# A transformer block with mixture-of-experts: the last two experts' rows added by matmuls from a gate matrix, the other pairs read back earlier, two norms from one power step, the mixer's scale folded into its weights

## What is computed

```python
# experts: token t goes to its two best experts of one group
ys = lax.ragged_dot(silu(xs @ w1) * (xs @ w3), w2, group_sizes) * gate   # 512 (token, expert) pairs
ffn = jax.ops.segment_sum(ys, tok, num_segments=256)                     # two rows per token are added
x = x + gate2 * ffn
...
x = rmsnorm(x, final_norm_w)                                             # end of the first block
h = rms_norm(x, norm_mix_g)                                              # second block: a second norm on it
d = causal window means (2, 4, 8, 16 tokens) of h, minus h               # per group of 256 columns
x = x + pool_scale * (einsum('bsgc,gcd->bsgd', d, pool_w) + pool_b)
x = x + conv_ffn(rms_norm(x, norm_ffn_g))                                # 1024 -> 2 x 2816 -> 1024
```

## Time and profile before

| what | value |
| --- | --- |
| median of 3 executions | 1063.36 us (1061.33 to 1064.96) |
| the profiled execution | 1059.67 us, its span 1057.8 us |
| mean granted TensorE clock of it | 0.952 of full speed |
| PE, DVE, ACT, POOL busy | 85%, 35%, 19%, 17% of the span |
| DMA, experts' stage | 1.0 of the 16 engines, some 400 to 415 GB/s |

### The profile page before, as it was taken

One profiled execution on the slowest core, in us unless ns is written; L12 is line 12 of the kernel. 1 busy time (PEld: TensorE's weight loads), 2 busy tenths in 40 slices (PEclk: granted clock), 3 DMA queues, 4 the chain that ended last, 5 costly groups with the idle time before them and its releaser, 6 DMA issues.

```text
span 1057.8 us, 11605 instructions
## 1 busy us (share of the span) xinstructions
PE 894.7 (85%) x4729; PEld 543.5 (51%) x4729; DVE 365.5 (35%) x639; ACT 199.5 (19%) x296; POOL 176.5 (17%) x187
## 2 busy tenths in 40 slices
PE   5679999999955979998887887887887279999998
PEld 2567756774432434433332332332322269999987
DVE  1244412232251242221221211212212566888843
ACT  2106212111130000000000000000000335565532
POOL 0000654011011120111101111011000221323300
PEclk9889999989987998999999999999999579999999
DMA  9898327364595999999999999999994784654511
GB/s 352 207 208 227 110 80 231 88 238 168 199 415 197 401 407 403 402 401 399 409 403 416 415 402 410 404 412 413 405 419 203 261 255 145 204 163 169 213 58 40
DMA packets 90803, 300.25 MB, mean 284 GB/s; under 512 B 12843, under 2 KB 36963, under 8 KB 66039
## 3 DMA queue, kind: packets, MB, share of 16 engines
q1 hardware_dynamic: 82727, 286.63, 72.7%
q10 hardware_dynamic: 2896, 8.58, 2.1%
q0 software_dynamic: 5120, 4.22, 1.4%
HBM read 300.44 MB, written 11.53 MB: 295 GB/s over the span
## 4 chain that ended last, share of the span: by engine, by line
PE 57%; DMA 33%; SPq 3%; issue 2%; DVE 2%; ACT 1%; POOL 1%; ACTq 0%; POOLq 0%; DVEq 0%
DMA arena<-in_w_dram 16%; DMA ring<-in_w_dram 13%; PE ps L421 9%; PE ps L763 7%; PE ps L847 6%; PE ps L849 6%; PE ps L848 6%; PE ps L410 5%; PE ps L766 4%; PE ps L786 3%; PE ps L483 3%; SPq L1874 2%; PE ps L431 2%; DMA rows_scratch<-MX 1%; DMA ring<-in_w_ada_dram 1%
## 5 line engine op out<-in xcount | busy, mean ns | idle before, releaser
L766 PE MATMUL ps<-ring,proj 128*64 128x512 f32 x288 | 134.1, 613 | 24.9 <-DMA ring<-in_w_dram 24.9
L763 PE MATMUL ps<-ring,proj 128*64 128x512 f32 x304 | 143.1, 612 | 1.7 <-issue 1.7
L1235 DVE TENSOR_TENSOR proj<-RQ,ps 64x512 f32<-64x512 f32 x32 | 22.1, 690 | 298.3 <-ACT RQ L1570 288.4
L766 PE MATMUL ps<-arena,proj 128*64 128x512 f32 x224 | 100.9, 596 | 20.6 <-DMA arena<-in_w_dram 20.6
L1570 ACT ACTIVATE RQ<-ps 64x512 f32<-64x512 f32 x32 | 18.9, 591 | 472.2 <-PE ps L766 472.2
L1800 POOL DMA_INDIRECT pair_scratch<-MX,idx x32 | 32.4, 1014 | 423.7 <-DVE MX L1249 423.7
L847 PE MATMUL ps<-h_h,w_h 128*128 128x256 f32 x352 | 100.8, 286 | 1.6 <-DVE h_l L1331 1.6
L849 PE MATMUL ps<-h_h,w_l 128*128 128x256 f32 x352 | 100.5, 286 | 0.0
L848 PE MATMUL ps<-h_l,w_h 128*128 128x256 f32 x352 | 100.5, 286 | 0.0
L421 PE MATMUL ps<-ring,hT 128*128 128x512 f32 x224 | 99.7, 601 | 0.8 <-ACT hT L1522 0.8
L763 PE MATMUL ps<-arena,proj 128*64 128x512 f32 x208 | 95.1, 596 | 1.9 <-issue 1.9
(11 more groups left out here) (285 smaller groups left out, 1377.6 us busy)
## 6 DMA issues: line engine op xcount, KB each, us to landing
ring<-in_w_dram SPq DMA_DIRECT2D x108, 1024.0 KB, 28.0
arena<-in_w_dram SPq DMA_DIRECT2D x84, 1024.0 KB, 28.1
ring<-in_w_ada_dram SPq DMA_DIRECT2D x12, 2048.0 KB, 10.0
ring<-in_ffn_w_in_dram SPq DMA_DIRECT2D x22, 1024.0 KB, 7.7
ring<-in_w_in_dram SPq DMA_DIRECT2D x8, 2048.0 KB, 22.3
ring<-in_ffn_w_out_dram SPq DMA_DIRECT2D x5, 2048.0 KB, 8.1
ring<-in_w_out_dram SPq DMA_DIRECT2D x2, 2048.0 KB, 9.8
rows_scratch<-MX ACTq DMA_DIRECT2D x4, 512.0 KB, 11.5
```

Source lines behind the costliest of these rows:

```text
L763: pe.matmul(ps[0:SLOTS, :], XTe[i % 2][:, k, :], u1[:, k, :], start=(k == 0), stop=(k == 7))
L766: t = pe.matmul(ps[64:64 + SLOTS, :], XTe[i % 2][:, k, :], u3[:, k, :], start=(k == 0), stop=(k == 7))
```

## The change

The last two experts (30 and 31) are no longer scattered. In the `aside` DVE builds from the slots and the gates a matrix `spread` (tokens by slots, for each of the two experts and each half of the tokens), PE transposes it, and DVE copies it out (`spread_t`). After `down(31)` PE multiplies `spread_t` by the buffers `YS`, eight matmuls with 64 rows of contraction, into four PSUM banks, and DVE adds these to `X`. The other pairs are read back by ACT once expert 29's rows have landed, ahead of `silu(31)`, into slot 0 of `ring`, and DVE adds them within the experts' loop: the first half of the tokens ahead of its `down(30)`, the second ahead of its `down(31)`. Since rows of the last two experts' pairs are never written, both scratch tensors are zeroed in the first part by eight transfers of 512 KB from a zeroed row buffer.

The second norm's sum is expressed by the first's, so that POOL takes both powers in one instruction on two columns. The preparations (L1660 before) move to DVE. POOL multiplies `pool_w` by the scale, in place, behind the powers, and DVE's separate multiplication goes. Bands and `pool_w` share slot 1 and are loaded as soon as `up(30)` has used it. Two matmuls of 128 columns become one of 256.

```diff
             for blk in range(1, NBLK):
                 places(blk)
+            ps = take("spread")
+            pe.wait_ge(spread_ready, 1)
+            for j in range(2):
+                for n in range(2):
+                    i = pe.transpose(ps[:, 256 * j + 128 * n:256 * j + 128 * n + 128], spread[:, j, n, :], ident)
+            i.then_inc(*mm.up("spread"))
...
+            acc = {(n, q): take("x2", n, q) for n in range(2) for q in range(2)}
+            for j, i in enumerate(LAST):
+                pe.wait_ge(*drained("down", i))
+                for n in range(2):
+                    for q in range(2):
+                        r = slice(64 * q, 64 * q + 64)
+                        t = pe.matmul(acc[n, q][:, :], spread_t[r, j, n, :], YS[i % 4][r, :], start=(j == 0), stop=(j == 1))
+                        if j:
+                            t.then_inc(*mm.up("x2", n, q))
...
-                pe.matmul(ps[:, 0:128], MX[:, 0, cc], band[:, g, 0:128], start=True, stop=True)
-                pe.matmul(ps[:, 128:256], MX[:, 0, cc], band[:, g, 128:256], start=True, stop=False)
+                pe.matmul(ps[:, 0:256], MX[:, 0, cc], band[:, g, 0:256], start=True, stop=False)
...
             def aside():
                 ve.tensor_copy(fcol, full("fcol")[:, 0:192]).then_inc(*free("fcol"))
+                for n in range(2):
+                    for k in range(2):
+                        ve.tensor_scalar(share[:, n, k, :], flat[k][:, n, NE - 2:NE], gate[:, k, n:n + 1], None,
+                                         ALU.mult).then_inc(*vd.up())
+                ve.wait_ge(*vd.now())
+                for j in range(2):
+                    for n in range(2):
+                        for k, to in enumerate((spread, spread_2)):
+                            ve.tensor_scalar(to[:, j, n, :], cst("places"), slot[:, k, n:n + 1], share[:, n, k, j:j + 1],
+                                             ALU.is_equal, ALU.mult).then_inc(*vd.up())
+                ve.wait_ge(*vd.now())
+                ve.tensor_tensor(spread, spread, spread_2, ALU.add).then_inc(spread_ready, 1)
                 for blk in range(1, NBLK):
                     places(blk)
+                ve.tensor_copy(spread_t, full("spread")[:, :].rearrange("p (e n t) -> p e n t", e=2, n=2)).then_inc(*free("spread"))
...
+                if add_pairs and i in LAST:
+                    add_pairs(i - LAST[0], (pairs_in[i - LAST[0]], 32))
                 down(i)
...
+            second_residual(0)
+            second_residual(1)
+            mean_squares(0)
+            both_norms(0)
+            mean_squares(1)
+            both_norms(1)
...
+                    ve.tensor_tensor(X[:, n, gs], X[:, n, gs], full("pooled", n, gg)[:, :], ALU.add).then_inc(*free("pooled", n, gg))
+            for n in range(2):
+                ve.wait_ge(third_sq, n + 1)
+                ve.tensor_scalar(tms[n][0][:, 0:1], ss[:, n:n + 1], 1.0 / 1024, 1e-6, ALU.mult, ALU.add).then_inc(*vd.up("x3_mean", n))
             for n in range(2):
                 newton(rr[:, n:n + 1], [q[:, 0:1] for q in tms[n]])
...
+            def main_pairs():
+                all_scattered(ac, main, NE - 2)
+                read_pairs(ys, pairs_in)
...
+                if pairs and i == N - 1:
+                    pairs()
                 ac.wait_ge(*E.mm.of("up", i))
...
+            for n in range(2):
+                po.wait_ge(*vd.of("means", n))
+                root(tms[n][1][:, 0:2], pair_m[n])
+            w_pool = mixer_weights()[1].rearrange("p (g c) d -> p g c d", c=2)
+            po.wait_ge(*filled(("mixer",)))
+            po.tensor_tensor(w_pool, w_pool, v_psc.rearrange("p (g d) -> p g d", g=4).unsqueeze(2).to_broadcast(
+                [128, 4, 2, 256]), ALU.mult).then_inc(pool_scaled, 1)
...
+            sp.wait_ge(row_zeroed, 1)
+            for i in range(4):
+                for pairs in (ys, ys_more):
+                    sp.dma_start(pairs.rearrange("(p a) c -> p (a c)", p=128)[:, 1024 * i:1024 * i + 1024],
+                                 v_pb).then_inc(pairs_zeroed, 16)
             load_ada(4)
...
-            sp.wait_ge(pairs_in[1], 32)
-            sp.wait_ge(pairs_in[0], 32)
...
+            s, _ = units.at["mixer",]
+            sp.wait_ge(*used(units.before["mixer",]))
```

More of the change, by code:

```diff
@@ L721, in tensor_program @@
                 pe.wait_ge(*more.mm.now())
+                for b in range(8):
+                    pe.wait_ge(more.bank_free[b], more.banks.count[b])
+            acc = {(n, q): take("x2", n, q) for n in range(2) for q in range(2)}
[7 more added lines that the diff above has]
+                            t.then_inc(*mm.up("x2", n, q))
             tensor_last(pe, take)
@@ L1207, in vector_program, with vector_experts @@
             with ve.If(some > 0):
-                vector_experts(ve, more, None)
-                ve.wait_ge(*more.drained("down", len(more.jobs) - 1))
+                vector_experts(ve, more, None, None)
+                ve.wait_ge(more_pairs_in, 64)
+                for n in range(2):
+                    for k in range(2):
+                        ve.scalar_tensor_tensor(X[:, n, :], YP[:, k, n, :], gate[:, k, n:n + 1], X[:, n, :], ALU.mult,
+                                                ALU.add).then_inc(*more_vd.up())
+                        ve.wait_ge(*more_vd.now())
             vector_last(ve, full, free, newton)
-        def vector_experts(ve, E, aside):
+        def vector_experts(ve, E, aside, add_pairs):
             def full(*name):
@@ L1255, in vector_experts @@
             else:
[L1256 to L1257 removed]
+                all_scattered(ve, main, NE - 2)
             turn_x(0)
@@ L1282, in add_second, with mixer_weights, second_residual @@
+        def mixer_weights():
+            w = slots[units.at["mixer",][0]]
+            return w[:, 0:1536].rearrange("p (g c) -> p g c", g=4), w[:, 2048:4096].rearrange("p (a b) -> p a b", b=256)
+        def vector_last(ve, full, free, newton):
+            def second_residual(n):
+                for q in range(2):
+                    xq = X[:, n, 512 * q:512 * q + 512]
+                    ve.tensor_tensor(xq, xq, full("x2", n, q)[:, :], ALU.add).then_inc(*free("x2", n, q))
                 ve.wait_ge(finals_in, 48)
+                ve.wait_ge(*drained("x2", n, 0))
+                ve.wait_ge(*drained("x2", n, 1))
@@ L1781, in gpsimd_program @@
                 gpsimd_experts(po, more, None)
-                for i in range(4):
-                    po.wait_ge(more.scattered[i], 16 * (len(more.jobs) // 4))
-            for i in range(4):
-                po.wait_ge(main.scattered[i], 16 * (NE // 4))
-            po.memset(mark, 0.0).then_inc(joined, 1)
-            gpsimd_last(po, row_power, power)
+                all_scattered(po, more, len(more.jobs))
+            all_scattered(po, main, NE - 2)
+            gpsimd_last(po)
         def gpsimd_experts(po, E, aside):
@@ L1817, in gpsimd_experts, with gpsimd_last, root @@
                     gather(i + 4)
-                scatter(i)
+                if E is main and i == 0:
+                    po.wait_ge(pairs_zeroed, 128)
+                if E is more or i not in LAST:
+                    scatter(i)
                 if aside and i == 3:
                     aside()
-        def gpsimd_last(po, row_power, power):
-            def again(n):
-                po.wait_ge(*vd.of("norm_once", n))
-                power(1.0 / 1024, 1e-6, sv[:, n:n + 1], [q[:, 4:5] for q in tms[n]])
-            row_power("x2_sq", 0, n=0)
-            again(0)
-            row_power("x2_sq", 1, n=1)
-            again(1)
+        def gpsimd_last(po):
+            def root(y, m):
+                po.tensor_tensor(y, m, half.to_broadcast([128, m.shape[1]]), ALU.pow).then_inc(pow_ready, 1)
+            for n in range(2):
+                po.wait_ge(*vd.of("means", n))
[4 more added lines that the diff above has]
+                [128, 4, 2, 256]), ALU.mult).then_inc(pool_scaled, 1)
             src = ffn_part(0)
```

164 lines of the change are left out of this document (80 added, 84 removed).

## The result

The changed kernel takes 1064.89 us (median of 19 runs, 1062.78 to 1070.9), the kernel before beside it 1061.57 us (19 runs, 1056.27 to 1066.22). The ratio is 1.0034, with a 95% interval of 1.002 to 1.0047: the change costs 3.6 us, between 2.1 and 5.0. The forecast was +4.3 us, and with it 1067.7 us (range 1059 to 1072); the level is 2.8 us too high, most of it because the 1063.36 us it starts from, the median of three executions, lie 1.8 us above the median of 19.

What follows compares the result with a forecast made beforehand. The weight stream bounds the experts' stage, then a serial chain up to the feed-forward part; +4.6 (aside) - 0.85 (join) + 0.5 + 0.1 = +4.3 us on 1063.36 gives 1067.7 us, range 1059 to 1072.

Steps and rivals of the forecast that it cites:

- What bounds it, first part: Weight stream bounds the experts' stage; eight more transfers early on cost zero, up to 10.5 us if uncovered.
- The aside: Behind down(3), the matrix work makes PE resume 5.3 us later, leaving the weight stream dry for 4.6 us.
- rival C: The stream has a reserve, so the aside costs nothing; with the join as forecast -0.3 us, 1063; chance 0.13.
- The dip forecast for about 410 us: Sign in the new profile: DMA share well under 1 for some 4 us around 410 us.
- The join: Serial chain from the last experts to the mixer, rebuilt around the pairs' readback: a net gain of 0.85 us.
- 817.8: Time in us when the first half's pairs are read back, delayed by SP's full queue; down(31) then starts at 821.7.
- the first half is complete at 831.1, and DVE goes through: Behind down(31): spread matmuls finish, DVE's additions follow directly; PE starts the mixer 11.7 us after down(31), at 839.7.
- Mixer and third norm: Merged matmuls zero (0 to 0.5 gain), 0.5 us lost to POOL's pool_w multiplication, third norm's chain zero.
- The lock: At the mixer, POOL's pool_w multiplication locks DVE's second newton out of the shared port: 0.5 us lost.
- A: The forecast itself, aside and join as calculated: 1065 to 1070 us; chance 0.45.
- B: First pairs in by 814, clock stays full, mixer 7 to 9 us earlier: -4 to -2, 1059.5 to 1062; chance 0.2.
- D: Early pairs and a reserve in the stream together: -8 us, about 1055.5; chance 0.1.

Runs made afterwards that it cites:

- experiment 5: Changed kernel, but SP issues the mixer's and feed-forward's weights only once both halves of the pairs are read back; ratio to the kernel before 1.0061.
- no_branch: Changed kernel with the route for overflowing experts left out on VectorE alone; ratio to the kernel before 1.0003.
- asked_early: plain_best, with TensorE and VectorE asking about overflow ahead of the last two experts' work; 1056.53 us, ratio to the kernel before 0.9949.
- order_fix: Changed kernel, GpSimd multiplying pool_w ahead of the powers and the third norm's first Newton step directly behind its mean; ratio to the kernel before 1.005.
- before_aside: Kernel before, with the gate matrix built, turned and copied in its aside but never used; ratio to the kernel before 1.0027.
- pairs_behind: Changed kernel, but VectorE adds both halves' pairs behind its down(31) instead of ahead of down(30) and down(31); ratio to the kernel before 1.002.
- best1: Changed kernel with the edits of gate_late, pairs_behind and order_fix together; ratio to the kernel before 0.9975.
- gate_late: Changed kernel, gate matrix built behind down(5) and turned behind down(7), only the slots copied in the aside; ratio to the kernel before 1.0001.
- plain_best: Changed kernel with the edits of gate_late and pairs_behind, and ScalarE issuing the readback behind silu(31); 1058.52 us, ratio to the kernel before 0.9969.

## Why the prediction was right or wrong

**What bounds it, first part.** Right for the experts' stage, which moved with the stream and by the stream's loss. That the eight more stores cost nothing is not shown, only that it is little: the load of modulation weights behind them is issued at 100.1 to 103.6 us in the ten kernels that have them, 101.8 on average, and at 100.7 and 100.8 in the two without, so about 1 us is not excluded. Of the 5.2 us by which the profiled execution of the changed kernel is late at the aside, 1.4 are there at that load, and 3.8 arise between 253 and 291 us, which no run explains.

**The aside.** Right, and the largest term: forecast 5.3 us longer for TensorE and 4.6 for the stream, measured 4.9 and 4.3. The rival C (a reserve in the stream) has fallen by experiments 1 and 2: put into the kernel before, the same work cost 4.5 us of the stage; taken out of the changed one, it gave back 3.9. The dip forecast for about 410 us lies at 412 to 418, in an execution whose aside began 5.2 us later.

**The join.** The steps up to down(31) held. From the wait for w3: silu(31) was to be 1 us later and starts at 817.55, 4.3 us behind it (3.7 in the earlier trace rows: 807.41 against 803.7), so 0.6 later; the first addition of pairs after 14.1, measured 13.9; down(31) after 18.0, measured 17.7; TensorE idle for 7, measured 7.20; the row groups of the spread side by side, 3.7 us for 16 records. That the new loads stand beside the readback was the reason given for 817.8, and experiment 5 makes it the smaller part, 1.1 us; the larger is probably the tail of w2(31), which no run took away. Two times in this walk don't follow from the terms beside them. The scatter's landing at 806.2 would be 805.7 (799.30 + 6.4), and 831.1 for the first half would be 830.4 at the latest (828.0 + 0.7 + 1.7). Both were near what came: the first read is issued 6.8 us after the scatter begins (815.66 against 808.83), and in no_branch, where nothing but the matmuls holds VectorE up, its first spread addition begins 2.85 us after the first spread matmul (833.82 against 830.97).

down(31) took 5.4 us instead of 6.3, as the clock was back after 834 us (0.88 between 834 and 836 and full in the next matmuls): a term too large by 0.9.

**The step that failed** is "the first half is complete at 831.1, and DVE goes through": the prediction walks VectorE from the last multiplication to the spread additions as if nothing lay between them. Between them lies the question about overflow. It lay at the same place in the kernel before, behind 817.87, and the prediction read past it because it cost nothing there: VectorE waited until 828.40 for the pairs anyway, 9.8 us, and a gap of 5.5 us is hidden in that. (Its trace has four transfers on q14 from 819.7 to 823.7, but doesn't say whose they are; all engines ask there.) The change took this wait away, and the jump came out from under it. Its price in this stretch is 3.5 us in the changed kernel, by no_branch, and 5.3 us once the rest of the chain is short, by asked_early; the medians of the whole time show 2.5 and 2.0 us of that. That the forecast of the tail (36.0 us from w3 to the mixer, measured 37.9) is off by only 1.9 comes from terms that were too large: down(31) starts 0.3 us sooner than forecast and takes 0.9 less, and from its end to the mixer it is 14.9 us instead of 11.7, which are the jump's. So the join cost 1.1 us where it was to bring 0.85.

**Mixer and third norm.** The lock is there as forecast, and the SBUF page of the Trainium skill ("SBUF — State Buffer", section "SBUF: two separate sides"), by which a VectorE instruction with two inputs in SBUF and a GpSimd instruction exclude each other for a whole instruction, agrees with this trace: a step of 0.16 us took 4.45, beginning 0.06 us after a GpSimd instruction of 4.50 and ending with it. Its price was forecast at 0.5 us and is 0.65 by order_fix, which also gained the third norm nothing. The stage as a whole is unchanged (25.19 and 25.23), and the trace shows what made up for the lock: from the mixer's first matmul to the first one behind its first group it is 6.14 us, with the wait of 0.60 in it, against 6.54 before. The granted clock is 1.00 from 4 us after that first matmul (855.19), in the kernel before only from about 6 (846.55). Whether the merging of the matmuls does this is open: before_aside, whose mixer is that of the kernel before, also needs only 6.10 us there. From the last result of the mixer to the second transposes it is 6.1 us (866.77 to 872.89), forecast 6.3.

**The sum.** +4.6 - 0.85 + 0.5 + 0.1 = +4.3 was forecast. The stages say +4.3 + 1.1 + 0 = +5.4, the whole times +3.6 (2.1 to 5.0). Runs of one kernel spread over 8 to 10 us, and they do so with the mean granted clock of TensorE in the run: at a clock of 0.952 or 0.953 the kernel before takes 1058.8 us on average (14 of 87 runs), at 0.941 to 0.943 it takes 1064.7 (12 runs). The changed kernel at 0.952 or 0.953 takes 1064.0 (10 of its 19 runs), 5.1 us more than the one before at the same clock. But it has that clock oftener, so that its median lies less than 5 us above. That would account for the 1.8 us between stages and medians; why it has that clock oftener is open, and so is whether the change itself brings it. That the forecast of the whole came so near was therefore in part luck: terms that were too large made up for some of the missing jump, and the 1.8 us by which the whole time lies under the stages for the rest.

Of the rivals, A was right in its place and its size. B named the mechanism of the join correctly, the arrival of the pairs, but not what would be left of it: pairs_behind takes the wait away and wins 3.3 us, not the 7 to 9 that B promised, because the jump is next. D could therefore not have given -8 either; best1, which does what D describes, is at -2.7.

## What to carry to other kernels

A wait that a change removes may have covered something that is no operation: list what the engine's program has between the two instructions, jumps over unused routes too, and give each a price before calling the gap closed. A jump belongs where its engine waits for something long in any case; here that took 5.3 us out of the stretch that held it, and 2.0 us of 1060 by the medians. And work for a later step should not make TensorE wait in a stage whose slots have just run dry: the same comparisons cost 4.3 us behind down(3), where TensorE waits for them, and at most 0.5 when VectorE makes them behind down(5) and TensorE comes for them two experts later. No run tells what they would cost behind down(5) with TensorE waiting.

## What the runs showed of the hardware

A jump over a route that isn't taken, with the load of its flag, costs VectorE 5.0 to 5.6 us (5.57 in after, 5.04 in gate_late, 5.06 in order_fix, 5.41 in pairs_behind, 5.48 in best1, 5.60 in plain_best) and TensorE 3.6 to 4.2 (pairs_behind, best1, plain_best). The timeline has only "issue" for it, and the instruction queues one small transfer 2.0 to 2.8 us ahead of its end. For TensorE it is followed by a second price: in best1 the spread matmuls behind the pause take 5.40 us, with a granted clock of 0.57 between 824 and 828, against 3.70 in gate_late, where no such pause stands ahead of them.

VectorE's additions of 128x1024 with three operands take 1.31 us each (5.24 for four) and, with GpSimd multiplying beside them for 4.49 us, 9.44 for the four: the two engines' times all but add up (9.73).

The readback of 512 KB pieces that took 4.5 us on idle DMA engines took 11.5 us from ScalarE's first issue to VectorE's start (815.66 to 827.18) behind the last expert's weights, and 10.5 (816.16 to 826.64) with only these ahead of it.
